# Smaller first pieces, a bank of its own for the first value unit, and a new row order in the output projections

## The reference

```python
def moba_mixer(xn, w_qkv, w_o, cos, sin):          # stage A; 256 tokens are one block
    qkv = (xn @ w_qkv).reshape(B, S, 3, N_HEADS, HEAD_DIM)
    q = apply_rope(qkv[:, :, 0], cos, sin)
    k = apply_rope(qkv[:, :, 1], cos, sin)
    o = moba_attention(q, k, qkv[:, :, 2])
    return o.reshape(B, S, N_HEADS * HEAD_DIM) @ w_o

def conv_ffn(xn, w_gate, conv_w, conv_b, w_up, w_down):
    g = xn @ w_gate
    gc = conv_b + sum(conv_w[j] * gp[:, j:j + S] for j in range(CONV_WIDTH))
    return (gelu(gc) * (xn @ w_up)) @ w_down
```

## Time and profile before

| | us |
|---|---|
| median of 3 runs | 1162.36 (1162.0 to 1164.17) |
| the profiled execution, its own time | 1162.03 |
| its span in the trace | 1160.2 |
| PE busy in the span | 1121.6 (97%) |
| DVE busy | 797.1 (69%) |
| ACT busy | 594.8 (51%) |
| DMA, share of 16 engines | 47.8% |

### The profile page before, as it was taken

One profiled execution on the slowest core, in us unless ns is written; L12 is line 12 of the kernel. 1 busy time (PEld: TensorE's weight loads), 2 busy tenths in 40 slices (PEclk: granted clock), 3 DMA queues, 4 the chain that ended last, 5 costly groups with the idle time before them and its releaser, 6 DMA issues.

```text
span 1160.2 us, 21441 instructions
## 1 busy us (share of the span) xinstructions
PE 1121.6 (97%) x9266; PEld 1095.0 (94%) x9266; DVE 797.1 (69%) x1180; ACT 594.8 (51%) x809; POOL 4.7 (0%) x10
## 2 busy tenths in 40 slices
PE   4999999999999999999999899999999989999998
PEld 4898999999998799999999899999999879999998
DVE  5876578776557777877657697774558756977741
ACT  5465456454347665554445365454447644654530
POOL 0000000000000000000001000000000000000000
PEclk9999999999999999999999899999999999999999
DMA  7443246555445045655553175555555423755540
GB/s 293 166 149 119 97 151 218 177 180 197 164 148 197 20 169 186 218 172 183 198 179 143 41 250 182 182 170 205 191 171 169 132 110 111 253 181 182 168 175 21
DMA packets 30238, 191.98 MB, mean 165 GB/s; under 512 B 4289, under 2 KB 5441, under 8 KB 9921
## 3 DMA queue, kind: packets, MB, share of 16 engines
q1 hardware_dynamic: 30144, 190.62, 47.8%
HBM read 189.56 MB, written 1.05 MB: 164 GB/s over the span
## 4 chain that ended last, share of the span: by engine, by line
PE 91%; DVE 5%; ACT 2%; issue 1%; DMA 1%; SPq 0%; ACTq 0%; DVEq 0%
PE bank L336 29%; PE bank L337 28%; PE bank L338 28%; DVE wlo L1294 2%; PE TB L455 1%; ACT whi L893 1%; PE bank L475 1%; DMA raw<-in_a_qkv 1%; PE SB L781 1%; PE SB L787 1%; PE SB L440 1%; PE SB L442 1%; PE SB L370 1%; PE bank L479 1%; PE bank L557 1%
## 5 line engine op out<-in xcount | busy, mean ns | idle before, releaser
L1294 DVE TENSOR_TENSOR wlo<-raw,whi 128x2048 fp32r<-128x2048 f32 (+2 forms) x183 | 402.4, 2202 | 107.8 <-ACT whi L893 107.8
L336 PE MATMUL bank<-xx,whi 128*128 128x256 f32 x1408 | 400.2, 284 | 6.0 <-DVE xx L1299 6.0
L338 PE MATMUL bank<-xx,wlo 128*128 128x256 f32 x1408 | 399.4, 284 | 0.0
L337 PE MATMUL bank<-xx,whi 128*128 128x256 f32 x1408 | 399.4, 284 | 0.0
L893 ACT ACTIVATE whi<-raw 128x2048 fp32r<-128x2048 f32 (+2 forms) x183 | 335.8, 1839 | 100.5 <-PE bank L338 94.3
L336 PEld LDWEIGHTS bank<-xx,whi 128*128 128x128 f32 x1408 | 271.3, 193 | 6.2 <-issue 6.2
L337 PEld LDWEIGHTS bank<-xx,whi 128*128 128x128 f32 x1408 | 271.3, 193 | 0.0
L338 PEld LDWEIGHTS bank<-xx,wlo 128*128 128x128 f32 x1408 | 271.2, 193 | 0.0
L336 PE MATMUL bank<-hx,whi 128*128 128x256 f32 x704 | 199.2, 283 | 0.0
L337 PE MATMUL bank<-hx,whi 128*128 128x256 f32 x704 | 199.2, 283 | 0.0
L338 PE MATMUL bank<-hx,wlo 128*128 128x256 f32 x704 | 199.2, 283 | 0.0
(11 more groups left out here) (149 smaller groups left out, 1247.7 us busy)
## 6 DMA issues: line engine op xcount, KB each, us to landing
raw<-in_gate SPq DMA_DIRECT2D x44, 1024.0 KB, 4.9
raw<-in_up SPq DMA_DIRECT2D x44, 1024.0 KB, 4.9
raw<-in_down SPq DMA_DIRECT2D x32, 1024.0 KB, 4.9
raw<-in_a_qkv SPq DMA_DIRECT2D x12, 1024.0 KB, 5.9
raw<-in_down SPq DMA_DIRECT2D x16, 768.0 KB, 4.3
raw<-in_d_qkv SPq DMA_DIRECT2D x12, 1024.0 KB, 4.9
raw<-in_a_o SPq DMA_DIRECT2D x4, 1024.0 KB, 4.9
raw<-in_b_o SPq DMA_DIRECT2D x4, 1024.0 KB, 5.1
```

The costliest lines, as they stand in the source:

```text
L336: e.matmul(po, ah, bh, start=start, stop=False, skip_group_check=True)
L337: e.matmul(po, ah, bl, start=False, stop=False, skip_group_check=True)
L338: return e.matmul(po, al, bh, start=False, stop=stop, skip_group_check=True)
L1294: e.tensor_tensor(wlo[n % RING][:, 0:nk * w], raw[n % RAW][:, 0:nk * w], whi[n % RING][:, 0:nk * w].bitcast(F32), ALU.subtract).then_inc(s ...
```

## The change

1. **Pieces.** `x` is loaded in four quarters instead of two halves, units 0 and 1 in four quarters each (128x512, 256 KB), and ACT and DVE split them by quarters. The quarters of `x` and of unit 0 alternate. `con` is issued ahead of unit 2. PE takes unit 0 row by row for both halves of the tokens (`first_keys`, in DD too, there on whole units), and in A unit 1 likewise (`first_queries`), with `norm_sums` after its seventh row. ACT runs one small Exp before its first wait for data. `squares` and `add_squares` are mixed into the quarters of unit 1.
2. **Bank.** `qkv_bank` gives the values of group 0 bank 3, so that their matmuls don't wait for `s_ev`.
3. **Order in A.** PE does `turn_over(0, 1)` after `half(1, 0, 0)`, not before `half(0, 2, 1)`. ACT does `value(0)` ahead of `hi(u+6)` and `turned_over(0, 1)` behind it. DVE does `lo(3)` after `rotated(0, 1)` instead of before `norm_col`. ACT copies the keys of group 3 ahead of `exponentials(5)`.
4. **Projection.** In the tails of A and DD, seven rows of unit 2 are done before row 7 of units 0 and 1, and unit 2's last row after it.

```diff
-            e.dma_start(xT[:, 0:4, :], dram["x"][:, 0:4, :]).then_inc(s_x, 16)
-            load(0)
-            e.dma_start(xT[:, 4:8, :], dram["x"][:, 4:8, :]).then_inc(s_x2, 16)
-            load(1)
+            for q in range(4):
+                at = slice(2 * q, 2 * q + 2)
+                e.dma_start(xT[:, at, :], dram["x"][:, at, :]).then_inc(s_x[q], 16)
+                load_quarter(0, q)
+            for q in range(4):
+                load_quarter(1, q)
+            e.dma_start(con[:, :], dram["con"]).then_inc(s_con, 16)
             load(2)
-            e.dma_start(con[:, :], dram["con"]).then_inc(s_con, 16)
...
+        def qkv_bank(s, g, i):
+            return bk(s, 3) if 3 * g + i == 2 else bk(s, (3 * g + i) % 2)
...
                 values(s, 7)
+                project(s, u, 2, range(7))
                 project_01(s, u, [7])
-                project_23(s, u)
+                project(s, u, 2, [7])
+                project(s, u, 3, range(8))
...
+                def first_keys():
+                    b = bk(s, 0)
+                    wh, wl = unit(u)
+                    if s:
+                        weights_here(u)
+                    for k in range(KD):
+                        x_here(s, k)
+                        if s == A and k % 2 == 0:
+                            quarter_here(0, k // 2)
+                        for h in range(2):
+                            sl = slice(h * 128, (h + 1) * 128)
+                            last = three(b[:, h * 256:(h + 1) * 256], xx[:, k, 0, sl], xx[:, k, 1, sl], wh[:, k, :],
+                                         wl[:, k, :], h == 0 and k == 0, k == KD - 1)
+                    last.then_inc(s_used, 1)
...
                 if s == A:
+                    first_queries()
                     half(0, 2, 0)
-                    turn_over(0, 1)
                     half(0, 2, 1)
                     half(1, 0, 0)
+                    turn_over(0, 1)
...
+                        if g == 2:
+                            turned_over(3, 1)
                         exponentials(s, j)
                         if j >= 2:
                             output_hi(s, j - 2)
-                        turned_over(g + 1, 1)
+                        if g < 2:
+                            turned_over(g + 1, 1)
...
+            e.activation(small[:, 0, 8:9], ones[:, 0:1], ACT.Exp)
             e.wait_ge(s_vec, 16)
-            e.wait_ge(s_x, 16)
-            for k in range(4):
-                split_x(A, k)
-            hi(0)
...
+            for q in range(4):
+                e.wait_ge(s_x[q], 16)
+                split_x(A, 2 * q)
+                split_x(A, 2 * q + 1)
+                hi_quarter(0, q)
+            for q in range(4):
+                hi_quarter(1, q)
+                squares(A, q)
...
                     rotated(0, 1)
+                    lo(u + 3)
                     lo(u + 4)
                     rotated(0, 0)
...
             lo(2)
-            lo(3)
             heads_mixer(A)
```

More of the change, by code:

```diff
@@ L105, in build @@
         s_raw = [sem(f"s_raw{i}") for i in range(RAW)]
-        s_con, s_x, s_x2, s_vec, s_win, s_bias, s_out = (
-            sem(f"s_{x}") for x in ("con", "x", "x2", "vec", "win", "bias", "out"))
+        s_first = [[sem(f"s_first{n}_{q}") for q in range(4)] for n in range(2)]
+        s_x = [sem(f"s_x{q}") for q in range(4)]
+        s_con, s_vec, s_win, s_bias, s_out = (
+            sem(f"s_{x}") for x in ("con", "vec", "win", "bias", "out"))
         s_hi, s_lo, s_used = sem("s_hi"), sem("s_lo"), sem("s_used")
+        s_hq, s_lq = sem("s_hq"), sem("s_lq")
         s_xh, s_xl, s_res = sem("s_xh"), sem("s_xl"), sem("s_res")
@@ L309, in sync_program, with load_quarter @@
             BIAS_AT = [first[DD] + 6, first[DD] + 7, first[DD] + 13, first[DD] + 16]
+            def load_quarter(n, q):
+                name, i, _, _ = plan[n]
+                at = slice(512 * q, 512 * q + 512)
+                e.dma_start(raw[n][:, at], dram[name][i][:, at]).then_inc(s_first[n][q], 16)
             e.dma_start(vec[:, :], dram["vec"]).then_inc(s_vec, 16)
-            e.dma_start(xT[:, 0:4, :], dram["x"][:, 0:4, :]).then_inc(s_x, 16)
-            load(0)
-            e.dma_start(xT[:, 4:8, :], dram["x"][:, 4:8, :]).then_inc(s_x2, 16)
-            load(1)
+            for q in range(4):
[5 more added lines that the diff above has]
+            e.dma_start(con[:, :], dram["con"]).then_inc(s_con, 16)
             load(2)
-            e.dma_start(con[:, :], dram["con"]).then_inc(s_con, 16)
             for n in range(3, N_UNITS):
@@ L341, in weights_here, with quarter_here @@
                 e.wait_ge(s_lo, n + 1)
+            def quarter_here(n, q):
+                if q < 3:
+                    e.wait_ge(s_lq, 3 * n + q + 1)
+                else:
+                    e.wait_ge(s_lo, n + 1)
             def x_here(s, k):
@@ L497, in project_01, with project @@
                             last.then_inc(s_used, 1)
-            def project_23(s, u):
-                for c in (2, 3):
+            def project(s, u, c, ks):
+                if ks[0] == 0:
                     weights_here(u + c)
-                    for k in range(KD):
-                        last = across(u + c, bk(s, c), k, ox, k, k == 0, k == KD - 1)
+                for k in ks:
+                    last = across(u + c, bk(s, c), k, ox, k, k == 0, k == KD - 1)
+                if ks[-1] == KD - 1:
                     last.then_inc(s_used, 1)
@@ L518, in heads_mixer, with first_queries @@
                 s_out_of = {A: s_ev, DD: s_cp}[s]
+                def first_keys():
[12 more added lines that the diff above has]
+                    last.then_inc(s_used, 1)
+                def first_queries():
+                    b = bk(s, 1)
+                    wh, wl = unit(u + 1)
+                    for k in range(KD):
+                        if k % 2 == 0:
+                            quarter_here(1, k // 2)
+                        for h in range(2):
+                            sl = slice(h * 128, (h + 1) * 128)
+                            last = three(b[:, h * 256:(h + 1) * 256], xx[:, k, 0, sl], xx[:, k, 1, sl], wh[:, k, :],
+                                         wl[:, k, :], h == 0 and k == 0, k == KD - 1)
+                        if k == 6:
+                            norm_sums(s)
+                    last.then_inc(s_used, 1)
                 def half(g, i, h):
                     n = u + 3 * g + i
-                    b = bk(s, (3 * g + i) % 2)
+                    b = qkv_bank(s, g, i)
                     if h == 0:
@@ L526, in half @@
                         if 3 * g + i == 1:
-                            e.wait_ge(s_res, n_res(s - 1, 1)) if s else None
-                        elif 3 * g + i >= 2:
+                            e.wait_ge(s_res, n_res(s - 1, 1))
+                        elif 3 * g + i > 2:
                             left, of = divmod(3 * g + i - 2, 3)
@@ L536, in half @@
                     for k in range(KD):
-                        if g == 0 and i == 0 and h == 0:
-                            x_here(s, k)
                         last = three(b[:, h * 256:(h + 1) * 256], xx[:, k, 0, sl], xx[:, k, 1, sl], wh[:, k, :],
@@ L566, in pair_scores @@
                                   for a in range(2)])
[L568 to L572, removed]
+                first_keys()
                 if s == A:
+                    first_queries()
                     half(0, 2, 0)
-                    turn_over(0, 1)
                     half(0, 2, 1)
                     half(1, 0, 0)
+                    turn_over(0, 1)
                     for g in range(3):
@@ L602, in heads_mixer @@
                             half(3, 2, 0)
-                    turn_over(3, 0)
+                            turn_over(3, 0)
                     transposes(s, 4)
@@ L613, in heads_mixer @@
                 else:
+                    norm_sums(s)
+                    half(0, 1, 0)
+                    half(0, 1, 1)
                     half(0, 2, 0)
@@ L831, in latent_mixer @@
                 project_01(s, u + 10, [6, 7])
-                project_23(s, u + 10)
+                project(s, u + 10, 2, range(8))
+                project(s, u + 10, 3, range(8))
             def pool_mixer():
@@ L889, in hi @@
                 _, _, nk, w = plan[n]
-                e.wait_ge(s_raw[n % RAW], 16 * (n // RAW + 1))
+                e.wait_ge(s_raw[n % RAW], 16 * (n // RAW + (n % RAW > 1)))
                 if n >= RING:
@@ L1019, in value @@
                 def value(g):
-                    b = bk(s, (3 * g + 2) % 2)
+                    b = qkv_bank(s, g, 2)
                     e.wait_ge(s_used, u + 3 * g + 3)
@@ L1038, in heads_mixer @@
                     hi(u + 5)
+                    value(0)
                     hi(u + 6)
                     turned_over(0, 1)
-                    value(0)
                     hi(u + 7)
@@ L1248, in pool_mixer, with hi_quarter @@
                     next_input(F2, g)
```

(32 more changed lines are left out.)

## The result

The changed kernel takes 1165.02 us (median of 9 runs, 1163.8 to 1166.52), the kernel before 1162.42 (9 runs, 1161.08 to 1164.23). The ratio is 1.0023 with a 95% interval of 1.0012 to 1.0033: slower by 2.6 us. The forecast was 1162.5 and no change that can be measured; 1165.02 lies inside its range, but at the upper end, and on the side of the rival in which the tails run at the lower clock.

What follows compares the result with a forecast made beforehand. PE, busy 97% of the span, was taken as the bound, so only its waits and lower-clock time could move. Terms -4.0 - 0.5 + 2.6 - 0.5 + 2.6 = +0.2 gave 1162.5 us, range 1159.3 to 1165.5.

Steps and rivals of the forecast that it cites:

- First matmul: Start of A: first weight quarter lands at about 5.9, so PE starts at 7.2 instead of 13.0 us.
- rival of slow pieces: Loads at start of A: pieces at half rate cost some 3 us, 1165.4, chance 0.08; extreme about 1175, chance 0.01.
- What is late next: Start of A: PE idle 4.8 us before unit 3, whose bank the DVE chain frees late; `turn_over(0, 0)` at 39.6.
- The start: Start of A as a whole: a gain taken as 4.0 us, with bounds of 2.6 and 5.8.
- The value bank: Start of A: with their own bank, the values let unit 2 follow without the 3.1 us wait.
- Group 3's keys: Copies of group 3: the 1.42 us key wait goes, the `qT` wait grows from 0.91 to 1.86; net -0.5 us.
- The tails: Tails of A and DD: chain 4.0 us later, waits of 1.65 and 2.05 in F0 and F3; +2.6 us each.
- The clock in the tails: Rival, tails of A and DD: paired waits lower PE's clock, up to 1.5 us more each, 1165.5 us; chance 0.11.
- DD's start: Start of DD: `first_keys` needs row 6 of x later, so the 0.51 us wait goes; -0.5 us.
- The sum: Whole kernel: the terms for start, keys, both tails and DD's start add to +0.2 us, forecast 1162.5 us.

Runs made afterwards that it cites:

- halves: `tail_back` with x, unit 0 and unit 1 loaded in halves instead of quarters, splits and matmuls still in quarters: 1161.91 us, ratio 0.9989 to the kernel before.
- tail_rows: The changed kernel with two rows of unit 2 ahead of row 7 in A's tail and four in DD's, instead of seven: 1158.87 us, ratio 0.9973.
- bank_back: `tail_back` with the values of group 0 in bank 0 again instead of their own bank: 1158.66 us, ratio 0.9966 to the kernel before.
- tail_only: The kernel before with only the new row order of the projection in the tails of A and DD: 1170.3 us, ratio 1.0072.
- kt_back: `tail_back` with ACT copying group 3's keys behind `exponentials(5)` again: 1160.56 us, ratio 0.9983 to the kernel before.
- start_order: `tail_back` with DVE doing `lo(4)` behind the second rotation instead of ahead of it: 1158.37 us, ratio 0.9966 to the kernel before.
- two_rows: The kernel before with only two rows of unit 2 put ahead of row 7 in the tails of A and DD: 1161.21 us, ratio 0.9992.
- tail_back: The changed kernel with the old order of the projection's rows in the tails of A and DD: 1159.4 us, ratio 0.9982 to the kernel before.

## Why the prediction was right or wrong

**First matmul.** 7.2 forecast, 8.64 in this profile, 7.33 to 8.21 in the six kernels with the same pieces. The step that failed is the landing of the first weight quarter at 5.9, counted back with 315 to 415 GB/s. ACT's row says when it came:

```profile
7.14 0.63 ACT L1311 ACTIVATE whi<-raw 128x512 fp32r<-128x512 f32 x1 [1.45 <-DMA raw<-in_a_qkv]
```

The rate at that time was 217. In the six others ACT began this quarter at 5.84 to 6.71, so that 5.9 holds in the earliest of them alone. This is the rival of slow pieces in small. For full bandwidth the Trainium skill asks for at least 1 MiB per DMA ("DMA: Bandwidth & Descriptors", Rules for kernel authors). The lower rate of the pieces, 217 to 285 GB/s against 373 to 379, agrees with that. Larger pieces were not the better choice for all that: `halves` was slower than the quarters.

**What is late next.** Right in kind and size. The wait at unit 3 was 4.70, forecast 4.8; `turn_over(0, 0)` came at 41.02, forecast 39.6. The norm factor began at 22.20 and not at 20.7. ACT's and DVE's rows for unit 2, and the norm factor's:

```profile
17.46 1.92 ACT L948 ACTIVATE whi<-raw 128x2048 fp32r<-128x2048 f32 x1 [0.56 <-DMA raw<-in_a_qkv]
19.41 2.29 DVE L1358 TENSOR_TENSOR wlo<-raw,whi 128x2048 fp32r<-128x2048 f32 x1 [1.78 <-ACT whi L948]
22.20 0.16 DVE L1398 TENSOR_SCALAR small<-SB 128x2 f32<-128x2 f32 x1 [0.50 <-PE SB L391]
```

Unit 2 landed at 17.4 and not at 16.5, so that `lo(2)` ended at 21.7 and not at 20.7; PE's sums, late with the first matmul, added the last 0.5. The first of the two is the larger part. In `tail_rows` the first matmul was at 7.33, nearly as forecast, and the norm factor still began only at 22.05, behind this row of DVE, with `turn_over(0, 0)` at 41.01, no earlier than here:

```profile
19.84 2.29 DVE L1359 TENSOR_TENSOR wlo<-raw,whi 128x2048 fp32r<-128x2048 f32 x1 [2.17 <-ACT whi L949]
```

The start gave 2.9 us, the sum had 4.0: a term mis-sized by when the loads landed, unit 2 above all.

**The value bank** was counted as what takes the 3.1 us wait away. `bank_back` shows no gain from it: the wait is the chain's, wherever PE meets it.

**Group 3's keys.** -0.5 forecast, -0.5 measured (-2.9 to -3.4 in the table); the new wait is 2.04, forecast 1.86.

**The tails.** The mechanism, its places and its size were right: the chain 4.0 us later, waits of 1.65 and 2.05 forecast and of 1.49 and 1.88 measured. A tail was to cost 2.6; DD's cost 2.8 (-1.0 up to F3, +3.8 in it).

**The clock in the tails.** This rival, with a chance of 0.11, came true in half. In F0 it cost 1.5 us more, so that A's tail cost 4.3. The step that failed is its condition, "it decides from somewhere between 1.9 and 3.1 us of wait". F3 has the same two waits and no low clock; `tail_only` shows it in both; and in `kt_back` it goes with waits of 1.4 and 0.9. Waits of that size went with a low stretch in some executions and not in others: it should have been a term of the sum with a mean, and not a rival with a threshold. The nine runs of the changed kernel agree: a mean granted clock of 0.991 in three with a mean of 1166.4 us, 0.994 in four with a mean of 1164.1.

**DD's start.** -0.5 forecast, -0.75 measured. **F2's first unit** was not forecast at all. PE comes back from its 6.0 us wait inside a low stretch of 6.8 us, of which 4.8 us were left before the change and 3.1 after it. From there to the end of 96 matmuls it took 13.85 us before (643.37 to 657.22) and 13.1 after (644.34 to 657.43). How much is left after the wait depends on when the stretch began; nothing in the change aims at that.

**The sum.** -2.9 for the start, -0.5 for the keys, +4.3 for A's tail, -0.75 for F2, -0.75 for DD's start and +2.8 for DD's tail make +2.2; the spans differ by 2.0, the medians by 2.6. Against the forecast's +0.2, the start is 1.1 short and A's tail 1.7 over, and F2, DD's start and DD's tail give 0.8 back. Two errors on the same side carried the median just over the 2.3 us that I had called no change. That it still lies within the range is in part luck: without F2's 0.75, which I hadn't forecast, it would have been near 1165.8, above the range's 1165.5.

## What to carry to other kernels

Work put ahead of a row that waits delays also what waits for that row to be finished: here 42 matmuls (5.1 us) covered a wait of 0.93 us, with 1.7 us of spare time in the chain behind, and brought waits of 3.4; 12 matmuls (1.45 us) covered it and brought none. Cover a wait with no more than it needs, and read the spare time at the far end of the chain. And when an instruction is moved whose end releases a load, follow the load to its user, as `start_order` shows.

## What the runs showed of the hardware

The granted clock fell to 0.50, the 1.2 GHz level, for stretches of 3.4 or 6.8 us. Such a stretch came with every wait of 3.1 to 5.1 us at the start of A (nine of the eleven profiles have one), and with none of the 2.17, 2.39 and 2.50 there in `tail_only`, `two_rows` and `start_order`. With waits of 0.9 to 2.1 us it came in some: 0.73 in `tail_back` from 104 to 110, 1.00 in the kernel before around its 1.42 and 0.91. So the length of the wait alone doesn't tell it. A stretch of 3.4 us costs about 1.5. From 4 to 8 us of the program, loads in pieces of 256 KB came at 217 to 285 GB/s (seven profiles) and in pieces of 512 KB at 233 (one), where a load of 512 KB with the 1 MB units behind it came at 373 to 379 (three). This I had not expected from a trace in which the first loads ran at 315 to 415.
